# Up weights of experts 7 to 14 loaded over ScalarE's DMA queue instead of SyncE's

## The reference

```python
def hier_moe(x, ...):                       # x: 256 tokens x 2048
    # top-1 of 4 groups, then top-2 of the 4 experts inside it -> gate[token, expert]
    h = silu(einsum("td,edf->tef", xt, w_gate)) * einsum("td,edf->tef", xt, w_up)
    y = einsum("tef,efd->td", h * gate[:, :, None], w_down)
# w_gate, w_up: 16 x 2048 x 512, w_down: 16 x 512 x 2048, float32, per layer
```

## Time and profile before

| | us |
|---|---|
| median of three runs | 1404.32 (1403.17 to 1404.77) |
| the profiled execution | 1405.07 |
| its span in the profile | 1402.9 |
| TensorE busy | 1340.2 (96%) |
| ScalarE busy | 429.1 (31%) |
| VectorE busy | 549.9 (39%) |
| queue q1 (SyncE's loads) | 477.50 MB, 85.1% of the 16 DMA engines |
| queue q10 (ScalarE's loads) | 2.65 MB, 0.5% |

### The profile page before, as it was taken

One profiled execution on the slowest core, in us unless ns is written; L12 is line 12 of the kernel. 1 busy time (PEld: TensorE's weight loads), 2 busy tenths in 40 slices (PEclk: granted clock), 3 DMA queues, 4 the chain that ended last, 5 costly groups with the idle time before them and its releaser, 6 DMA issues.

```text
span 1402.9 us, 22192 instructions
## 1 busy us (share of the span) xinstructions
PE 1340.2 (96%) x8981; PEld 758.6 (54%) x8981; DVE 549.9 (39%) x887; ACT 429.1 (31%) x643; POOL 41.8 (3%) x35
## 2 busy tenths in 40 slices
PE   9899999999898989999999999999999999889897
PEld 8634444333443448888888877773434444334343
DVE  5813223222231336566665655561322323223132
ACT  5511111110111127665656564531111111011111
POOL 1200000000000000000000000110000000000000
PEclk9999999999999999999999999999999999999999
DMA  9999999999999999554545444569999999999996
GB/s 361 392 416 421 420 420 422 422 422 422 422 422 422 420 401 338 183 167 159 179 133 195 152 150 147 183 240 399 420 420 421 421 422 421 421 422 422 421 420 268
DMA packets 93946, 481.58 MB, mean 343 GB/s; under 512 B 7618, under 2 KB 7828, under 8 KB 44476
## 3 DMA queue, kind: packets, MB, share of 16 engines
q1 hardware_dynamic: 93292, 477.50, 85.1%
q10 hardware_dynamic: 432, 2.65, 0.5%
q0 software_dynamic: 160, 0.52, 0.1%
HBM read 478.56 MB, written 2.10 MB: 343 GB/s over the span
## 4 chain that ended last, share of the span: by engine, by line
issue 53%; PE 30%; DMA 11%; DVE 3%; POOL 1%; ACT 1%; SPq 0%; DVEq 0%; POOLq 0%; ACTq 0%
PE ps L1583 12%; DMA ring<-in_moe_w_up 11%; PE ps L1427 7%; PE ps L1625 5%; PE ps L1508 2%; PE ps L1545 1%; POOL head_rs L561 1%; PE ps L1546 1%; DMA resid<-in_x 1%; DVE ws L926 1%; DVE ps L1201 0%; DVE resid L1204 0%; PE ps L1448 0%; DVE rest L940 0%; PE ps L1610 0%
## 5 line engine op out<-in xcount | busy, mean ns | idle before, releaser
L1583 PE MATMUL ps<-ring,xg 128*64 128x512 f32 x1920 | 441.8, 599 | 36.0 <-DMA ring<-in_moe_w_up 30.4
L1427 PE MATMUL ps<-ws,xs 128*128 128x512 f32 x1632 | 385.5, 395 | 7.4 <-DVE xs L1352 2.4
L1427 PEld LDWEIGHTS ps<-ws,xs 128*128 128x128 f32 x1632 | 305.2, 189 | 76.2 <-DVE ws L929 4.1
L1583 PEld LDWEIGHTS ps<-ring,xg 128*64 128x64 f32 x1920 | 142.1, 137 | 304.5 <-issue 304.4
L1625 PE MATMUL ps<-ring,hidT 128*64 128x512 f32 x960 | 212.9, 595 | 0.0
L929 DVE SCALAR_TENSOR_TENSOR ws<-ring,vecs,ws 128x512 fp32r<-128x512 f32 x192 | 134.4, 748 | 87.7 <-ACT ws L582 87.7
L582 ACT ACTIVATE ws<-ring,vecs 128x512 fp32r<-128x512 f32 x192 | 127.4, 716 | 83.5 <-PE ps L1427 83.5
L1110 DVE TENSOR_TENSOR y_lo<-ps,y_hi 64x512 fp32r<-64x512 f32 x112 | 77.1, 689 | 191.6 <-ACT y_hi L644 189.0
L1089 DVE TENSOR_TENSOR resid<-resid,ps 128x512 f32<-128x512 f32 x112 | 72.0, 684 | 169.8 <-PE ps L1546 169.8
L1625 PEld LDWEIGHTS ps<-ring,hidT 128*64 128x64 f32 x960 | 66.2, 137 | 122.9 <-issue 121.5
L644 ACT ACTIVATE y_hi<-ps 64x512 fp32r<-64x512 f32 x112 | 66.4, 593 | 209.2 <-PE ps L1625 207.2
(11 more groups left out here) (180 smaller groups left out, 720.5 us busy)
## 6 DMA issues: line engine op xcount, KB each, us to landing
ring<-in_moe_w_gate SPq DMA_DIRECT2D x120, 1024.0 KB, 20.3
ring<-in_moe_w_up SPq DMA_DIRECT2D x120, 1024.0 KB, 22.3
ring<-in_moe_w_down SPq DMA_DIRECT2D x120, 1024.0 KB, 21.7
ring<-in_w_kv SPq DMA_DIRECT2D x32, 1024.0 KB, 5.7
ring<-in_w_q SPq DMA_DIRECT2D x16, 1024.0 KB, 5.2
ring<-in_w_o SPq DMA_DIRECT2D x16, 1024.0 KB, 5.1
extra<-in_moe_w_gate SPq DMA_DIRECT2D x8, 1024.0 KB, 12.4
extra<-in_moe_w_up SPq DMA_DIRECT2D x8, 1024.0 KB, 11.2
```

The lines of the kernel that those rows point to most:

```text
L1427: last = mm(ps[:, bank + t, :], xs[:, px, k, cols], ws[:, b, pw, j, :], start=(first and j == 0 and n == 0), stop=(last_unit and j == 1 an ...
L1583: last = mm(ps[CAP * h:CAP * h + CAP, b, :], xg[:, b, k, :], both[h][:, j, :], start=(k == 0), stop=(k == KD - 1))
```

## The change

SyncE no longer loads the up weights (parts 1, 3, 5 and 7) of experts 7 to 14 in either layer; ScalarE loads them, over its own queue. That is 4 MB of 12 for each of 8 experts in each of 2 layers: 64 loads of 1 MB. ScalarE waits, as SyncE did, until the up quarter of the expert before has been read, so each load still becomes possible at the same event. The four waits and loads for expert e+1 stand in ScalarE's program just ahead of `expert_in` of expert e, e = 6 to 13. SyncE's loop runs over experts instead of pairs, with experts 6 and 15 complete. ScalarE's loop over pairs is cut in two: pairs 0 to 2 without loads, pairs 3 to 6 with them. Slots, semaphores, their counts, and the order on TensorE, VectorE and GpSimd stay as they are.

```diff
+        SHARED = (2 * PEELED + 3, EXP - 1)
+        BY_ACT = (1, 3, 5, 7)
...
-                with sp.Fori(PEELED + 1, NPAIR) as i:
-                    for b in range(2):
-                        for m in range(SLOTS):
-
-                            n = n1 + PAIR_SLOTS + SLOTS * b + m
-                            sp.wait_ge(slot_read, PAIR_SLOTS * (NPAIR * l + i) + SLOTS * (b - 1) + m + 1)
-                            sp.dma_start(ring_view(n, m), expert_load(l, 2 * i + b, m)).then_inc(slot_loaded[n % SLOTS], 16)
+                def expert(e, others=()):
+
+                    for m in range(SLOTS):
+                        if m not in others:
+                            sp.wait_ge(slot_read, SLOTS * (EXP * l + e - 1) + m + 1)
+                            sp.dma_start(ring_view(n1 + m, m), expert_load(l, e, m)).then_inc(slot_loaded[(n1 + m) % SLOTS], 16)
+
+                expert(SHARED[0] - 1)
+                with sp.Fori(*SHARED) as e:
+                    expert(e, BY_ACT)
+                expert(SHARED[1])
...
-                with act.Fori(0, NPAIR - 1) as i:
+                n1 = START_MOE[l] + RING_OF[AHEAD]
+
+                def two_experts(i, loads):
                     for b in range(2):
+                        for m in BY_ACT if loads else ():
+                            act.wait_ge(slot_read, n0 + SLOTS * (2 * i + b) + m + 1)
+                            act.dma_start(four(n1 + m), w_up_v[l, 2 * i + b + 1, m // 2]).then_inc(
+                                slot_loaded[(n1 + m) % SLOTS], 16)
                         expert_in(i, b)
...
+                with act.Fori(0, PEELED + 1) as i:
+                    two_experts(i, False)
+                with act.Fori(PEELED + 1, NPAIR - 1) as i:
+                    two_experts(i, True)
```

## The result

The changed kernel takes 1420.06 us (median of four runs, 1415.21 to 1421.73), the kernel before 1403.74 in the same sitting (four runs, 1400.53 to 1404.77). The ratio is 1.0116, with a 95% interval of 1.0099 to 1.0132: 16.3 us slower, between 13.9 and 18.5. The direction is the one forecast, and the time lies in the stated range. The profiled execution took 1415.21 us (span 1413.0), the shortest of the four. Lines have moved: L1583 is now L1601, L1625 is L1643, L1508 is L1526.

What follows compares the result with a forecast made beforehand. The expert stage was taken as set by the DMA engines, with a thin margin over TensorE. Layer 1's 5.8 and layer 0's 6.0 us made 11.8 on 1405.07, 1416.9; less 0.75 for the median, 1416.1 us, range 1404 to 1424 (8 in 10).

Steps and rivals of the forecast that it cites:

- The order of landing: Experts 7 to 14: queues alternate packet for packet, so up quarters overtake; in layer 1 down3(13) lands at 1337.8, not 1327.8.
- not a growing one: Experts 7 to 12: the same displacement in each, still 29.8 us per expert, nothing to be added.
- TensorE free 7.4 us late: End of expert 13, both layers: TensorE finishes with down3(13) 7.4 us later than before.
- named as possible at 2.5 us a load: Smaller displacement: each up quarter of expert 14 not in by 1337.8 takes 2.5 us a layer off.
- The 2.40 us of issue stay: Layer 1, gap ahead of expert 14: stays 2.40 us, as the loop is left in the same way.
- The waits of expert 15 absorb 1.6 and 1.4: TensorE's small waits at the stage's end go, taking 1.59 us (layer 1) and 1.39 us (layer 0) off its lateness.
- Attention gives nothing back: Attention after layer 0 starts 6.0 us late and recovers none, since no engine waits for a load in its first 120 us.
- The rate counted at 0: Expert stages: DMA rate with two queues in use stays as before, 0 us; bounds 5.6 us a layer either way.
- Two queues move bytes faster: Rival, chance 0.10: one queue's fixed packet time hides behind the other's data, 5.6 us a layer gained; 1393 us without overtaking.
- contention: Rival, chance 0.10: two queues pay the fixed packet time twice, 23.0 us in all, 1427 us.
- the rival with 1404.3 us: Order doesn't matter, chance 0.12: the stage is bound by bytes, and queues might be served in the order of issue.
- ScalarE's work counted at 0: ScalarE's four added loads per expert: 0 us taken, 0.5 us a layer if the cover of 0.6 us were gone.

Runs made afterwards that it cites:

- expert 14 alone: Changed kernel with ScalarE loading only expert 14's up quarters in both layers, SyncE those of experts 7 to 13: 1420.38 us, ratio 1.0125 to the kernel before.
- the first execution: First profiled execution of the unaltered changed kernel, the shortest of its four runs: 1415.21 us.
- the one near the median: A later profiled execution of the unaltered changed kernel, from its third timing: 1421.33 us.
- experts 7 to 13 alone: Changed kernel with ScalarE loading the up quarters of experts 7 to 13, SyncE those of 14 again: 1404.97 us, ratio 1.001 to the kernel before.
- expert 7 alone: Changed kernel with ScalarE loading only expert 7's up quarters in both layers: 1403.12 us, ratio 1.0002 to the kernel before.
- the second profile: Profile from the second timing of the unaltered changed kernel; that execution took 1416.14 us, the timing 1419.0 us, ratio 1.0118.
- two of 14: Changed kernel with ScalarE loading only the q0 and q1 up quarters of expert 14: 1405.86 us, ratio 1.0017 to the kernel before.
- the loads issued later: Changed kernel with ScalarE's four loads per expert moved behind `expert_in` and the copy after it: 1415.58 us, ratio 1.0084 to the kernel before.
- the downs: Changed kernel with ScalarE loading the down quarters of experts 7 to 14 instead of the up quarters: 1414.8 us, ratio 1.0079 to the kernel before.
- the layer-1 kernel: Changed kernel with ScalarE's up loads in layer 1 only (32 loads): 1410.85 us, ratio 1.0055 to the kernel before.
- two early, two late: Changed kernel with q0 and q1 up loads issued ahead of `expert_in`, q2 and q3 behind it: 1412.25 us, ratio 1.0064 to the kernel before.

## Why the prediction was right or wrong

*The order of landing* held. The shares were 289 to 288 packets, and the gate of q0(14) in layer 1 landed at 1343.62, 1347.88 and 1348.02 us in three executions (the changed kernel twice, expert 14 alone). Less the shifts of 3.64, 7.80 and 7.85 that is 1340.0, 1340.1 and 1340.2; 1340.3 was forecast. But not all four up quarters had landed ahead of down3(13), as the forecast has them: in layer 1 the last of them landed 3.45 us behind it in the first execution and 0.96 us behind it in the one near the median. Down3(13) landed 8.1 and 9.4 us late there, and 9.8 us late in the expert-14 kernel, where all four were in; 9.9 was forecast.

*The cost sits at expert 13 to 14 and nowhere else*, as forecast ("not a growing one"): expert 14 alone costs +17.5, experts 7 to 13 alone +1.4, expert 7 nothing.

*TensorE free 7.4 us late* held in part: 7.5 in layer 1 of the expert-14 kernel, 7.6 and 8.1 in two executions of the changed one; in layer 0, 8.7 in one of them, with the lower clock described below, and 6.9 with expert 14 alone. In the first execution it was 4.9 and 5.8, and 5.2 in layer 0 of the second profile: the downs came earlier there, which the forecast had named as possible at 2.5 us a load.

*"The 2.40 us of issue stay"* is the step that failed, and with it the start at 1339.5 + 2.40. The gap depends on how long down3(13) was in before TensorE read it. There are 28 places to look at, two layers in each of 14 profiles. In 13 of them this lead was 2.3 us or more (before, expert 7 alone, experts 7 to 13, two of 14, the loads issued later, the downs, and layer 0 of the layer-1 kernel); there the gap was 2.0 to 2.6 us, but for one place in which an up quarter was late. In the other 15 the lead was at most 1.0 us, and the gap was 3.0 to 4.8. In these the start keeps its distance from the landing of down3(13), 6.5 to 6.8 us: 6.77 and 6.74 in the first execution, 6.76 and 6.52 in the one near the median. Before, with a lead of 2.4 us, it was 6.73 and 6.66. What lies between landing and start is in the last section. The landing of the first gate of expert 14 does not decide: in layer 0 it lies 0.96 us apart in the two executions (460.91 and 461.87), down3(13) 2.20 us (456.88 and 459.08), and the start 2.19 us (463.65 and 465.84).

So the term that was mis-sized is the lateness of the start. The forecast made down3(13) 9.9 us late, took off 2.5 us because before the change this quarter was in 2.4 us ahead of its use, and carried 7.4 to the start. Those 2.4 us were not spare. Near the median down3(13) landed 9.4 us late in both layers, and the start was 9.4 and 9.3 us late. The first step of expert 14, which took up to 1.1 us longer (6.49, 6.17, 6.04 against 5.35), adds to it in some places.

*The waits of expert 15 absorb 1.6 and 1.4* held within 0.5 us: none is left in it (one block of 64 products), and in layer 1 of the first execution 8.2 - 1.6 = 6.6 stands against 6.1 measured; in layer 0, 7.2 + 1.1 of longer first step - 1.4 = 6.9 against 6.7.

*Attention gives nothing back* held: +0.2 us in the execution near the median, and 8.6 of 16.3 us come through it from layer 0. The 3.0 us that it gave in the first execution go with TensorE's clock: between the layers' expert products the granted clock was at half for 10.2 us before, for 10.2 near the median, and for 3.4 in the first execution.

*The rate counted at 0* held: 420 to 423 GB/s, and at most -0.3 to +3.1 us with 56 loads in the second queue. "Two queues move bytes faster" and "contention" each wanted 11 us. The Trainium skill, DMA: Bandwidth & Descriptors, "Issuing engines are not separate DMA queues", says that several issuing engines save only the sequencer's time. For the rate the trace agrees. Read as "the issuing engine makes no difference", which was the rival with 1404.3 us, it fails: the time rose by 1.2% at the same rate, with the order of landing changed.

*ScalarE's work counted at 0* held. An issue takes 0.4 us there; TensorE's gathering waited for `slot_scale` three times, 0.9 us in all from 1160 to 1400 us, each time ahead of downs that were waited for anyway. The expert-7 kernel carries the same four loads per layer at no cost.

*Sum.* Forecast 5.8 + 6.0 = 11.8. Near the median 8.1 + 7.6 = 15.7, with 0.6 elsewhere. The 3.9 between them are the two late starts, 9.4 - 7.4 and 9.3 - 7.4.

## What to carry to other kernels

In this kernel a second queue on busy DMA engines was not more bandwidth but another order: while both had work, each got half the packets, so the shorter queue overtook. Price a move by counting the loads that will go ahead of the one needed next, times the DMA time of one load (here 2.485 us), and look first where nothing comes after to catch up with; in the middle of this long stage the same displacement was free within 3 us. And do not carry a gap labelled "issue" over as a constant: find what it keeps its distance from. Here that was the last load that is waited for inside the loop, and its lead of 2.4 us over its use, which looked spare, was not.

## What the runs showed of the hardware

Between down3(13) and expert 14 the profile has a record that bears on the gap put to issue. The loop over pairs runs without any packet of the "instruction" kind on queue q8: in the kernel before the DMA view from 1100 to 1331 us has one queue only. The next such packet, of 16 KB, starts at 1331.78; below are the queues of 1100 to 1331 us, then the instruction queue in windows of 0.2 us or less around that packet's start, for the kernel before (from 1331.70), the first execution of the changed kernel (from 1343.50) and the one near the median (from 1348.80):
```profile
q1 hardware_dynamic: 13379, 97.43, 101.4%
```
```profile
q8 instruction: 1, 0.02, 34.3%
q8 instruction: 1, 0.02, 34.3%
q8 instruction: 1, 0.02, 45.8%
```

| us | down3(13) lands | instruction packet starts | TensorE free | expert 14 starts |
|---|---|---|---|---|
| before, layer 0 | 449.71 | 453.60 | 453.97 | 456.44 |
| before, layer 1 | 1327.84 | 1331.78 | 1332.10 | 1334.50 |
| first execution, layer 1 | 1339.58 | 1343.59 | 1341.56 | 1346.32 |
| near the median, layer 1 | 1345.05 | 1348.85 | 1347.49 | 1351.57 |
| two early, two late, layer 1 | 1335.34 | 1339.34 | 1338.24 | 1342.09 |
| experts 7 to 13, layer 1 | 1328.78 | 1335.14 | 1335.85 | 1337.87 |

Expert 14 starts 2.7 to 2.9 us behind the start of this packet in 27 of the 28 places; in the other one an up quarter was late (the version issued later, layer 1). The packet starts 3.7 to 4.0 us behind the landing of down3(13) in all 22 places in which this load was in at most 2.4 us ahead of its use, even where the products with it were slowed. In the six others, where it had been in for at least 3.5 us, the packet starts 1.2 to 1.7 us behind the first of those products. That TensorE waits here for its own next instructions is an inference from these constant distances: the profile doesn't say for which engine a packet is fetched. What sets the 3.7 to 4.0 us, no run separates.

TensorE's granted clock fell to half after some waits of 2.4 to 3.3 us and not after others of the same length. In the first profile of the changed kernel, a window over the products behind such a wait (columns as above), and the timeline:
```profile
1221.30:1224.70 3.40, 3.40 (x9) 0.89 (x11) 0.00 (x0) 0.00 (x0) 0.00 (x0) 0.50 1.01 422
```
```profile
1221.23 3.68 PE L1643 MATMUL ps<-ring,hidT 128*64 128x512 f32 x8 [3.05 <-DMA ring<-in_moe_w_down]
1224.70 4.83 PE L1601 MATMUL ps<-ring,xg 128*64 128x512 f32 x16
```
0.50 is the level of 1.2 GHz; eight products took 3.68 us instead of 1.94, and the step behind them 4.83 instead of 3.65. After a gap of 2.50 us in the kernel with two of expert 14's loads it stayed at full speed:
```profile
1339.80:1343.30 3.50, 3.50 (x16) 1.15 (x16) 0.90 (x2) 0.00 (x0) 0.00 (x0) 1.00 1.01 417
```
The first step of expert 14 before, 5.35 us after a gap of 2.40, is such a slowed step too, as its granted clock shows; and attention's first products, after a gap of 2.4 us before as after, ran slowed before and at full speed in the first one after:
```profile
1334.60:1339.80 5.20, 5.20 (x17) 1.66 (x17) 0.99 (x2) 0.00 (x0) 0.00 (x0) 0.67 1.02 421
522.30:525.30 3.00, 3.00 (x7) 2.45 (x8) 2.41 (x4) 0.52 (x2) 0.00 (x0) 0.50 1.05 385
```
```profile
528.95:531.75 2.80, 2.80 (x13) 2.25 (x13) 2.41 (x4) 0.52 (x2) 0.00 (x0) 1.00 1.05 387
```
Each such fall costs 1.6 to 1.7 us (5.35 against 3.65; 4.62 against 3.02 for the twelve first products of attention), and the same kernel has it in one execution and not in another. That is part of the 6.5 us between this kernel's fastest and slowest run, and a reason to settle differences of a few microseconds from several profiles and not from one.
